# One trunk layer on one core: finer events in a written order per engine, column-wise modulation chunks, projection tiles in quarters

## What is computed

```python
sh1, sc1, g1, sh2, sc2, g2 = adaln_mod(cond, ada_w, ada_b)  # silu(cond) @ w + b, w 1024 x 6144
h = rms_norm(x, norm1_g) * (1 + sc1) + sh1
z = h @ w_in                                                # 1024 x 2816
y_rwkv, s_new = rwkv7_bidir(z_shift, z_g, s0, p)            # 8 heads x 64, two directions
y_conv = conformer_conv(z_conv, p)                          # GLU, depthwise conv width 31, LayerNorm
x = x + g1 * (concat([y_rwkv, y_conv]) @ w_out)
h = rms_norm(x, norm2_g) * (1 + sc2) + sh2
x = x + g2 * hier_moe(h, p)                                 # top 2 of 8 experts in 1 of 4 groups
```

## Time and profile before

| | |
|---|---|
| median of the runs | 1225.67 us |
| profiled execution's own time | 1223.6 us |
| span in its trace | 1221.9 us |
| mean granted TensorE clock | 0.809 |
| PE, DVE, ACT, POOL busy | 926.2, 607.4, 286.8, 63.3 us |

### The profile page before, as it was taken

The page is one execution under the profiler, slowest core; times in us unless marked ns, Lnnn a source line. Parts: engine busy times, 40 slices in busy tenths (PEclk is TensorE's granted clock), DMA queues, the critical chain, the costliest instruction groups (busy, mean ns, idle before and its releaser), DMA issues.

```text
span 1221.9 us, 15392 instructions
## 1 busy us (share of the span) xinstructions
PE 926.2 (76%) x5899; PEld 574.8 (47%) x5899; DVE 607.4 (50%) x1286; ACT 286.8 (23%) x496; POOL 63.3 (5%) x55
## 2 busy tenths in 40 slices
PE   1699997999747788687676968896279987779654
PEld 1355655666446475566555743443234333224221
DVE  2326999455656867678776244534722111012006
ACT  2240000050533505417322143101011111001002
POOL 0000000001001000010010000001011111010000
PEclk9999998999757566575575698897579999889878
DMA  9845522111011101110112427410579999899533
GB/s 329 294 178 214 208 91 73 46 35 27 1 18 27 19 1 27 19 27 1 18 27 53 168 100 247 174 67 34 226 282 420 419 419 419 318 416 421 207 139 135
DMA packets 72744, 193.76 MB, mean 159 GB/s; under 512 B 42309, under 2 KB 42815, under 8 KB 58463
## 3 DMA queue, kind: packets, MB, share of 16 engines
q1 hardware_dynamic: 64416, 174.19, 38.1%
q0 software_dynamic: 5472, 10.53, 2.3%
q10 hardware_dynamic: 2783, 8.06, 1.8%
HBM read 181.80 MB, written 19.34 MB: 165 GB/s over the span
## 4 chain that ended last, share of the span: by engine, by line
PE 45%; DVE 28%; DMA 16%; ACT 5%; issue 4%; SPq 1%; ACTq 0%; DVEq 0%; POOLq 0%; POOL 0%
PE bank L544 8%; DMA arena<-in_expert_w_up 8%; PE bank L2106 8%; DVE arena L947 7%; PE bank L1518 4%; PE bank L2128 3%; PE bank L1231 3%; DVE arena L1035 2%; PE bank L1282 2%; PE bank L1250 1%; PE bank L1253 1%; DVE arena L1084 1%; DVE arena L1082 1%; PE bank L1187 1%; DMA arena<-winv 1%
## 5 line engine op out<-in xcount | busy, mean ns | idle before, releaser
L544 PE MATMUL bank<-arena 128*128 128x320 f32 x704 | 201.3, 446 | 12.2 <-DVE arena L436 3.8
L544 PEld LDWEIGHTS bank<-arena 128*128 128x128 f32 x704 | 135.8, 195 | 79.3 <-issue 28.0
L2106 PE MATMUL bank<-arena 128*64 128x512 f32 (+2 forms) x528 | 130.2, 651 | 32.2 <-DMA arena<-in_expert_w_up 31.3
L947 DVE SCALAR_TENSOR_TENSOR arena<-arena 128x655 f32<-128x655 f32 x116 | 104.6, 902 | 4.6 <-DVE arena L947 0.2
L2106 PEld LDWEIGHTS bank<-arena 128*64 128x64 f32 (+2 forms) x528 | 46.4, 149 | 114.5 <-issue 113.2
L2186 DVE TENSOR_TENSOR arena<-arena,bank 128x256 f32<-128x256 f32 x17 | 7.2, 422 | 158.0 <-ACT arena L2160 158.0
L2128 PE MATMUL bank<-arena 128*64 128x512 f32 (+2 forms) x264 | 65.8, 641 | 10.0 <-DVE arena L2189 10.0
L1518 PE MATMUL bank<-arena 128*128 128x512 f32 x160 | 73.2, 616 | 0.0
L907 ACT ACTIVATE arena<-bank 64x128 f32<-64x128 f32 (+1 forms) x68 | 19.9, 292 | 174.2 <-PE bank L1282 172.8
L1273 PE MATMUL bank<-arena 64*64 64x64 f32 x320 | 25.3, 300 | 42.2 <-DVE arena L1132 34.4
L1518 PEld LDWEIGHTS bank<-arena 128*128 128x128 f32 x160 | 31.2, 197 | 38.8 <-issue 38.8
(11 more groups left out here) (333 smaller groups left out, 1395.5 us busy)
## 6 DMA issues: line engine op xcount, KB each, us to landing
arena<-in_expert_w_gate SPq DMA_DIRECT2D x33, 1024.0 KB, 15.5
arena<-in_expert_w_up SPq DMA_DIRECT2D x33, 1024.0 KB, 19.6
arena<-in_expert_w_down SPq DMA_DIRECT2D x33, 1024.0 KB, 19.3
arena<-in_ada_w SPq DMA_DIRECT2D x12, 2048.0 KB, 10.4
arena<-in_w_in SPq DMA_DIRECT2D x22, 512.0 KB, 3.6
arena<-expert_rows SPq DMA_DIRECT2D x10, 512.0 KB, 7.3
arena<-in_x_sample SPq DMA_DIRECT2D x8, 512.0 KB, 5.9
arena<-in_w_out SPq DMA_DIRECT2D x1, 4096.0 KB, 14.8
```

The costliest lines, as they stand in the source:

```text
L544: mm = nc.tensor.matmul(psum[4 + 2 * (n % 2) + half][:, 0:HALF], wring[:, n % NWIN, k], hT[:, k, half * HALF:(half + 1) * HALF], start=(k ...
L947: chain(nc.vector.scalar_tensor_tensor(acc, src, w, acc, ALU.mult, ALU.add))
L2106: mm = nc.tensor.matmul(psum[2 + n % 2][r, :], xeT[:, n % 2, c, r], gu[:, :, c, :], start=(c == 0), stop=(c == KD - 1))
```

## The change

- **Modulation.** Blocks 4 to 11 are gone from the front and the projection. Their weights come as 32 chunks of 128 columns (512 KB, `adaw` on POOL, two buffers that lie over the convolution's). TensorE computes a chunk with the weights as stationary side and the two conditioning columns as moving side (`adac`), ScalarE copies two columns a chunk into `modT`; one transpose, one sum with the bias and two stores (`adafin`, `adast`) write `modrows` at the end of unit 3. The first four blocks are computed as before, from the new layout of `ada_w`.
- **Tiles in quarters.** `z_quarter` issues 8 of a tile's 32 matmul instructions (4 contraction steps of one half), so that other events can stand between quarters. `ZTILES` is reordered: six tiles of r, k, v that unit 0 needs are tiles 6 to 11.
- **Events split.** LoRA, norm, bonus, transposes, `mv` and the merges are one event per bank; `kp`, `ar`, `bk`, `scan` in parts; the inversion in ten pieces instead of five; the taps in groups of four.
- **Merges** are taken out by ScalarE instead of VectorE. Filling the first state is an event of its own (`st`). The eighth state update of a long unit, whose result nobody reads, is not in the lists.
- **Order.** `PLACES` and the sort go; each engine has a written list, of which the start of TensorE's and VectorE's for unit 1 stands below.
- SyncE's `final` waits for the modulation rows before it loads the gate rows and w_out.

```diff
-        ZTILES = [("lora", 12)]
-        ZTILES += [(n, 14 + j + 4 * (n == "cb")) for j in range(4) for n in ("cb", "ca")]
-        ZTILES += [("gate", 13)]
-        ZTILES += [("rkv", 4 * m + j) for i in (0, 2) for m in range(3) for j in (i, i + 1)]
+        ZTILES = [("lora", 12), ("cb", 18), ("ca", 14), ("cb", 19), ("ca", 15), ("gate", 13), ("rkv", 0), ("rkv", 1),
+                  ("rkv", 4), ("rkv", 5), ("rkv", 8), ("rkv", 9), ("cb", 20), ("ca", 16), ("cb", 21), ("ca", 17),
+                  ("rkv", 2), ("rkv", 3), ("rkv", 6), ("rkv", 7), ("rkv", 10), ("rkv", 11)]
-        def z_tile(n):
+        def z_quarter(n, q):
...
+            for k in ks[4 * (q % 2):4 * (q % 2) + 4]:
+                mm = nc.tensor.matmul(psum[4 + 2 * (n % 2) + half][:, 0:HALF], wring[:, n % NWIN, k],
+                                      hT[:, k, half * HALF:(half + 1) * HALF], start=(k == ks[0]), stop=(k == ks[-1]))
+            if q == 3:
+                mm.then_inc(s_zmm, 1)
...
+            "pe": (
...
+                   "z.18.0 z.18.1 lora_a0.1 z.18.2 lora_a1.1 z.18.3 lora_w0.1 z.19.0 lora_w1.1 z.19.1 z.19.2 z.19.3 "
+                   "ta0.0 z.20.0 ta1.0 z.20.1 merge_y1.0 z.20.2 norm1.1 norm0.1 z.20.3 merge_z1.0 z.21.0 merge_y0.0 "
+                   "z.21.1 adac.0 z.21.2 adac.1 z.21.3 merge_z0.0 adac.2 X.0.0 gram0.1 T.0.0 adac.3 S.0.0 turn_v0.1 "
...
+                   "gram1.2 merge_z0.1 turn_v2.2 gram2.2 X.1.0 bonus1.2 mv2.2 T.1.0 mv0.2 gram3.2 S.1.0 Y.1.0 X.1.1 "
...
+                   "T.2.4 mv3.3 S.2.4 Y.2.4 adac.17 norm1.4 X.2.5 adac.18 T.2.5 mv0.3 S.2.5 adac.19 X.2.6 adac.20 T.2.6 "
+                   "Y.2.5 adac.21 S.2.6 Y.2.6 adac.22 X.2.7 ta1.3 T.2.7 ta0.3 Y.2.7 merge_y1.3 turn_v1.4 turn_v0.4 "
...
+            "dve": (
...
+                   "scan1.0 z.9 shift_k.0 norm1.0 z.10 norm0.0 kn.0 ar0.0 kp0.0 z.11 kp1.0 kp2.0 z.12 ar1.0 bk0.0 T.0.0 "
...
+                   "inv0.0 tap.2.2 inv1.0 tap.2.3 inv2.0 tap.2.4 z.15 inv3.0 tap.3.0 inv4.0 tap.3.1 z.16 tap.3.2 inv5.0 "
...
+            "pool": ("scale.0 adaw.0 adaw.1 adaw.2 adaw.3 adaw.4 adaw.5 scale.1 adaw.6 adaw.7 adaw.8 adaw.9 adaw.10 "
...
+                if ev == "adaw":
+                    if u == 0:
+                        for stored in s_cst:
+                            pool.wait_ge(stored, 32)
...
+                    if u >= 2:
+                        wait_filled(pool, u - 2, "ad")
+                    pool.dma_start(adac[:, u % 2].rearrange("p k n -> p (k n)"), ins["ada_w"][16 + u]
+                                   ).then_inc(s_adac[u % 2], 16)
...
+                if ev == "adac":
+                    pe.wait_ge(s_adac[u % 2], 16 * (u // 2 + 1))
+                    wait_free(pe, u, "ad")
+                    for k in range(KD):
+                        mm = nc.tensor.matmul(psum[BANK["ad"]][:, 0:2], adac[:, u % 2, k, :], condP[:, k, 0:2],
+                                              start=(k == 0), stop=(k == KD - 1))
+                    mm.then_inc(s_summed, 1)
+                    continue
...
-                    cuts = [31, 26, 20, 14, 7, 0]
+                    cuts = [31, 29, 26, 23, 20, 17, 14, 11, 8, 4, 0]
...
+                    sp.wait_ge(s_modst, 32)
                     sp.dma_start(gateb, ins["gate_lora_b"][0]).then_inc(s_gateb, 16)
```

More of the change, by code:

```diff
@@ L199, in build @@
         set1_at = regr.at
+        regc = Region(conv_at, set1_at)
+        modT, adabias, modrow = regc.take(2, 32), regc.take(P), regc.take(P)
+        adac = regc.take(2, KD, P)
         set1 = unit_set()
@@ L229, in build @@
         s_adaw = [sem(f"ada_block_landed{b}") for b in range(NADA)]
-        s_adab = [sem(f"ada_bias_landed{b}") for b in range(2)]
+        s_adac = [sem(f"ada_chunk_landed{b}") for b in range(2)]
+        s_adab = sem("ada_bias_landed")
         s_win = s_egu = [sem(f"w_in_or_gate_up_landed{b}") for b in range(NWIN)]
@@ L233, in build @@
         s_xt = [sem(f"tokens_landed{b}") for b in range(TILES)]
-        s_modst = [sem(f"mod_block_stored{b}") for b in range(2)]
+        s_modst = sem("mod_rows_stored")
         d_self, a_self, g_self = sem("vector_step"), sem("scalar_step"), sem("pool_step")
@@ L299, in sp_front @@
             ada_load(3)
[L300 to L304, removed]
+            for n in range(2, NWIN):
                 win_tile(n)
@@ L698, in build @@
+                "merge_z0": [("z0", 0)], "merge_z1": [("z1", 1)]}
+        for _q in range(4):
+            USES[f"turn_bk{_q}"] = [(f"t{_q}", _q)]
+            USES[f"turn_v{_q}"] = [(f"v{_q}", _q)]
+            USES[f"mv{_q}"] = [(f"m{_q}", _q)]
+        USES["adac"], USES["adafin"] = [("ad", 3)], [("af", 3)]
         BANK = {use: bank for uses in USES.values() for use, bank in uses}
@@ L826, in act_mix @@
                     X = (XR, XK, VP[:, C:])[m]
-                    if u == 0 and m == 0:
-                        for stored in s_modst:
-                            act.wait_ge(stored, 64)
                     for eng_done in (s_zeva, s_zevd):
@@ L888, in act_mix @@
                             WB[r].rearrange("p n q j -> p n j q"), ACT.Copy), s_wcopy, 2 * u + k + 1)
-                    for h in range(2):
+                elif ev in ("ta0", "ta1"):
+                    for h in (int(ev[2]),):
                         wait_filled(act, u, f"ta{h}")
@@ L979, in dve_mix @@
                     chain.announce(ins_, s_shiftD, 3 * u + m + 1)
-                elif ev == "scan":
-                    for h in range(2):
+                elif ev in ("scan0", "scan1"):
+                    for h in (int(ev[4]),):
                         wait_read(dve, u, f"lw{h}")
@@ L986, in dve_mix @@
                             chain(ins_)
-                    chain.announce(ins_, s_cs, u + 1)
-                elif ev == "norm":
-                    for h in range(2):
+                    if ev == "scan1":
+                        chain.announce(ins_, s_cs, u + 1)
+                elif ev in ("norm0", "norm1"):
+                    for h in (int(ev[4]),):
                         wait_filled(dve, u, f"n{h}")
@@ L1038, in dve_mix @@
                             s_read[BANK[f"g{q}"]], read_count(u, f"g{q}"))
-                elif ev == "bonus":
-                    for h, part in enumerate(halves(u)):
+                elif ev in ("bonus0", "bonus1"):
+                    for h, part in ((int(ev[5]), halves(u)[int(ev[5])]),):
                         wait_filled(dve, u, f"b{h}")
```

356 lines of the change are left out of this document (144 added, 212 removed), and 72 rows, old and new, of the table ORDER.

## The result

The changed kernel takes 1220.3 us in the median (13 runs, 1208.5 to 1224.4), the kernel before 1225.7 (13 runs, 1223.9 to 1227.4): a ratio of 0.994, 95% interval 0.991 to 0.997. Faster, but by 5.4 us where 40 were forecast, and above the upper end of the range, 1214. The profiled execution took 1215.2 us with a span of 1213.4.

The account below looks back on a forecast made before the run. The prediction took TensorE to bound the projection and a loop through several engines the four periods. -39 (front), -5 (periods) and +4 (queues) made -40 us, from 1225.67 to 1186 us, range 1153 to 1214.

Parts of the forecast that it names:

- Part A, removal: Input projection: eight modulation blocks of 2.65 us each leave a full TensorE, 21.2 us off.
- Part B, first step: Projection's end and unit 0: first scan step at 320.9 us instead of 360.1, -39 us; ends -54 and -19.
- Part C, price of a chunk: TensorE in the four periods: 2.1 us a chunk, 61 us for 29 chunks; 4.3 kept as the other end.
- Part C, gain of the new order: Four periods: reordering gains 5 us in each of the first two, dropped state updates (2.8 us) included.
- Part C, ends: Four periods together: net change of -5 us could lie anywhere from -45 to +35.
- Does a fuller TensorE get its clock back?: Clock in the four periods: 0.50 was granted in a fully busy stretch, so no gain was counted.
- Part D: Load queues: chunk loads cause no wait; late w_out and convolution reloads cost +4 us, ends 0 and +9.
- The sum: Whole kernel: -39 - 5 + 4 = -40 us, 1183.6 for the profiled execution, plus 2.1 for the median, 1186.
- the second: Rival: chunks delay scan steps and the four periods become TensorE's, +25 instead of -5, 1216 us; chance 0.18.

Follow-up runs that it names:

- e4: Kernel before without its modulation blocks 4 to 11, nothing in their place; unit 0's first scan step at 348.5 us, 11.7 earlier than in the kernel before.
- e1: Changed kernel with 1 of the 8 products of each modulation chunk, loads and order kept; unit 4 starts at 651.8 us against 676.2.
- e10: e3 with only the first two of the 32 chunk loads, the rest read again; unit 4 starts at 648.7 us against e3's 653.6.
- e11: Kernel before with the merges y and z taken out of PSUM by ScalarE instead of VectorE; 1227.2 us, 1.002 of the kernel before.
- e5: e3 with the context unit's token shifts of r and k moved later; 1199.8 us, 0.978 of the kernel before.
- e2: Changed kernel with only the first two of the 32 chunk loads, the rest read again; unit 4 starts at 675.8 us against 676.2.
- e3: Changed kernel with each chunk's weights as moving side and the conditioning columns loaded, everything computed; 1194.9 us, 0.977 of the kernel before.
- e9: Changed kernel with SyncE's wait for the modulation table put behind the loads of w_out and the convolution; 1216.3 us, 0.991 of the kernel before.
- e8: e3 with SyncE's modulation wait behind the w_out and convolution loads, and gram3.1 ahead of shift_r.2 on VectorE; 1190.1 us, 0.9705 of the kernel before.

## Why the prediction was wrong, by its steps

The timeline of TensorE in the front of the changed kernel, for the first two points:

```profile
80.03 30.14 PE L514 MATMUL bank<-arena 128*128 128x320 f32 x111
...
142.59 6.24 PE L514 MATMUL bank<-arena 128*128 128x320 f32 x16 [4.14 <-DVE arena L416]
...
286.32 1.92 PE L1281 MATMUL bank<-arena 32*32 32x32 f32 x32 [9.96 <-ACT arena L876]
```

- **Part A, removal (-21.2 of TensorE's work):** right as work, and the tiles do follow each other without the gaps of 2.65 us: 111 instructions without a gap in 30.14 us, 8.7 us for a tile's 32 (first row above). Alone it would have given 11.7 (e4).
- **Part B, first step (320.9):** right, 321.6. Its idle terms were met in size too: 4.14 us in front of 142.59 for VectorE's bank copy, and 9.96 in front of the first transpose of unit 0's inverse at 286.32, where 5 and 7.5 were taken. All idle time from the first tile on is 15.4 us, where the sum had 15.3. Its split into removal and order is by difference (e4).
- **Part C, price of a chunk (2.1 us "whatever the clock"):** the step that failed. It measured 1.84 at full and 3.58 at half clock, the latter nearer the other end of 4.3. The row it rested on the earlier trace rows was taken at a clock of 0.89, and the stage that the chunks moved to has 0.6. The doubling of long products had been put aside because a chunk streams almost nothing. It streams two columns, but it loads 16 times 128, and the pitch of these loads went from 126 to 218 ns with the clock. (The two rows cited for the doubling, 8 instructions in 1.92 us and 4 in 3.71, give a factor of 3.9 an instruction, not 2: at 243.40 the instructions overlap. The record of a single one lasts 588 and 1057 ns.) Twenty-nine chunks are 94 us of TensorE in the periods, not 61; by e1 they cost 22 us net where +4 was allowed (3 and 1 in the third and fourth period). That is 18 of the 32 us by which the periods missed.
- **Part C, gain of the new order (5 us in each of the first two periods, with the dropped updates):** failed as well, by the other 14: e1 is 4.7 longer than before where -10 was taken. Three things are in it. Unit 1's preparation did not come forward as far as unit 0's first step (10.2 us, 4.7 of which come back at the end). Some 7 us are the loads beside the stores of the inverse, which part D had put at nothing. And the order itself shortened the three pitches by 6 to 8 us at most (e10, and e1 less its longer stores; single traces), with nothing from the merges when they are moved alone (e11). The sum had read its 5 us out of two lists without asking whether what became earlier was on the loop. Why e1's second pitch has 92 us and its third 79 stays open; e5 only showed that moving the context unit's shifts doesn't shorten it.
- **Part C, ends:** +35 does not come out of its terms. The sums above, 308.4 us, with 10 more a period are 348.4, which is +20.5; and with the 4.3 us that part A kept as the other end the work alone would be 372 us, +44. Neither end of the price reached the range.
- **"Does a fuller TensorE get its clock back?"** Counted as no, and right in the third period: 0.50 in 65 full microseconds.
- **Part D:** right in size for the changed kernel. Loads landed in 3.9 us and without them unit 4 starts no earlier (e2), but they did lengthen the stores of the inverse, to 3.8 and 5.0 us in the last two units, hidden there behind a full TensorE and not hidden in e1 and e3. The tail grew by 3.3 of the 4 allowed; the late w_out is part of it (a wait of 2.11 us that e9 removes), the rest is not shown.
- **The sum:** -39, -5, +4 were -38.6, +26.8, +3.3. That gives 1215 for the profiled execution, which is what it took. The median lies 5.1 above it, not 2.1: in this series the changed kernel's runs spread over 16 us, those of the kernel before over 3.5.
- **The rivals:** the second, periods that become TensorE's at +25, is nearest to what happened (+26.8), and was given 0.18. It had the mechanism for the third and fourth period, where TensorE is idle 4.7 and 2.9 us; in the first two it is idle 9.5 and 9.1. That its number is so near is in part luck: it still had 2.1 us a chunk and made up the rest by waits. The third period "84.2 of 85.1" was the hint. With 3.58 a chunk the same sum gives 64.8 + 21.5 = 86.3, 81.6, 99.0 and 84.4 us of TensorE against 82.6, 83.5, 85.1 and 76.7: too much in three periods of four. (Busy it was 83.7, 67.5, 102.6 and 74.7, so this sum too holds only roughly.) Worked out for both ends of the price, it would have said that only the lower end fits.

## What to carry to other kernels

Take the price of an added operation at the clock of the stage that it moves to, and where it can be either of two, sum the engine's work for both before choosing: work is hidden only while the engine's total stays below the loop's length. Products with two moving columns and 128 loaded ones were paid for by their weight loads here; turned round, so that the few columns are loaded and the weights stream, they cost less than half. A reordering is worth what the pitch of the loop loses, measured at one event that recurs every round, and not the idle time that it removes. And a queue of loads that no engine waits for can still lengthen a small store on the loop: look at that store's own time, with and without the loads.

## What the runs showed of the hardware that was not expected

- Weight loads of 128 fp32 columns, one after another with products of two columns, came every 126 ns at the granted clock of 1.00 and every 218 ns at 0.50.
- A 256 KB store from SyncE's queue took 2.0 us, and 3.7 to 5.7 in e1 and e3 where loads of 512 KB from POOL's queue were under way.
- In the changed kernel TensorE, busy in all of 65 us with chunks, other short products and the weight loads between them, was granted 0.50 throughout; in e3, with TensorE less busy, the third period had 0.70 against 0.60 in the changed kernel.
- The changed kernel varies most from run to run: 1208.5 to 1224.4 and 1215.0 to 1233.0 us in two series, with the granted clock (0.820 in both runs of 1208.5, 0.806 and 0.807 in those of 1222.8 and 1224.0). The kernel before varied by 3.5 us in one series and by 7 to 9 in the others, e3 by 10.8, e8 by 5.9.
